# Two reorderings in the recurrent steps of a hybrid decoder: ScalarE's copy of the turned keys and VectorE's choice of levels

## The reference, cut to what matters

```python
def step(state, inp):                       # one chunk of one head
    qt, kt, vt, lf = inp
    b = jnp.cumsum(lf, axis=2)
    diff = b[:, :, :, None, :] - b[:, :, None, :, :]
    decay = jnp.where(tri, jnp.exp(jnp.where(tri, diff, 0.0)), 0.0)
    att = jnp.einsum('bhtc,bhsc,bhtsc->bhts', qt, kt, decay)
    o = jnp.einsum('bhts,bhsv->bhtv', att, vt) + jnp.einsum('bhtc,bhcv->bhtv', qt * jnp.exp(b), state)
    b_last = b[:, :, -1:, :]
    new_state = state * jnp.exp(b_last[:, :, 0, :, None]) + jnp.einsum('bhsc,bhsv->bhcv', kt * jnp.exp(b_last - b), vt)
    return new_state, o
```

## Time and profile before

| | us |
|---|---|
| median of 3 runs | 2272.9 (2272.58 to 2273.27) |
| the profiled execution | 2272.83 |
| its span in the profile | 2271.0 |
| TensorE busy | 2218.8 (98%) |
| TensorE weight loads busy | 1789.6 (79%) |
| VectorE busy | 1136.0 (50%) |
| ScalarE busy | 867.4 (38%) |
| GpSimd busy | 155.1 (7%) |
| mean granted TensorE clock | 0.996 |

### The profile page before, as it was taken

The page is one execution under the profiler, slowest core; times in us unless marked ns, Lnnn a source line. Parts: engine busy times, 40 slices in busy tenths (PEclk is TensorE's granted clock), DMA queues, the critical chain, the costliest instruction groups (busy, mean ns, idle before and its releaser), DMA issues.

```text
span 2271.0 us, 29054 instructions
## 1 busy us (share of the span) xinstructions
PE 2218.8 (98%) x11971; PEld 1789.6 (79%) x11971; DVE 1136.0 (50%) x1802; ACT 867.4 (38%) x1321; POOL 155.1 (7%) x136
## 2 busy tenths in 40 slices
PE   7999999999999999999999999999999999999998
PEld 6888887877667888888888888878776778888887
DVE  4333344888767333343643333458887563333444
ACT  3232223555655323222532322245565453222234
POOL 0000021211001000011000000212200010000210
PEclk9999999999999999999999999999999999999999
DMA  5333333322212333333333333323222233333322
GB/s 154 101 95 97 92 93 89 97 57 76 75 43 79 112 98 97 99 92 98 92 94 96 99 93 93 93 73 98 75 63 65 70 86 100 93 102 98 90 86 70
DMA packets 383443, 202.65 MB, mean 89 GB/s; under 512 B 17104, under 2 KB 380496, under 8 KB 383312
## 3 DMA queue, kind: packets, MB, share of 16 engines
q1 hardware_dynamic: 383312, 200.80, 30.8%
HBM read 198.68 MB, written 2.10 MB: 88 GB/s over the span
## 4 chain that ended last, share of the span: by engine, by line
PE 85%; DVE 7%; ACT 3%; issue 2%; DMA 1%; SPq 0%; DVEq 0%; ACTq 0%
PE banks L246 24%; PE banks L247 24%; PE banks L248 24%; PE banks L273 2%; PE banks L274 2%; PE banks L279 2%; DVE lev L1019 1%; DMA w_raw<-in_cmp_v_w_dram 1%; PE banks L1281 1%; DVE att L1055 1%; PE banks L1268 1%; DVE w_lo L238 1%; PE banks L1302 1%; PE banks L1232 1%; ACT lev L909 1%
## 5 line engine op out<-in xcount | busy, mean ns | idle before, releaser
L238 DVE TENSOR_TENSOR w_lo<-w_raw,w_hi 128x1024 fp32r<-128x1024 f32 (+2 forms) x378 | 457.3, 1214 | 867.5 <-ACT w_hi L232 867.1
L246 PE MATMUL banks<-xhi,w_hi 128*128 128x512 f32 x1888 | 743.4, 394 | 1.4 <-DVE proj L991 1.1
L248 PE MATMUL banks<-xhi,w_lo 128*128 128x512 f32 x1888 | 735.8, 390 | 0.0
L247 PE MATMUL banks<-xlo,w_hi 128*128 128x512 f32 x1888 | 735.4, 390 | 0.0
L232 ACT ACTIVATE w_hi<-w_raw 128x1024 fp32r<-128x1024 f32 (+2 forms) x378 | 377.1, 1000 | 854.0 <-PE banks L248 830.2
L246 PEld LDWEIGHTS banks<-xhi,w_hi 128*128 128x128 f32 x1888 | 356.4, 189 | 77.5 <-issue 2.5
L248 PEld LDWEIGHTS banks<-xhi,w_lo 128*128 128x128 f32 x1888 | 354.5, 188 | 74.7
L247 PEld LDWEIGHTS banks<-xlo,w_hi 128*128 128x128 f32 x1888 | 354.8, 188 | 72.8 <-issue 1.4
L246 PE MATMUL banks<-hhi,w_hi 128*128 128x512 f32 x704 | 277.4, 394 | 0.0
L248 PE MATMUL banks<-hhi,w_lo 128*128 128x512 f32 x704 | 274.1, 389 | 0.0
L247 PE MATMUL banks<-hlo,w_hi 128*128 128x512 f32 x704 | 274.0, 389 | 0.0
(11 more groups left out here) (247 smaller groups left out, 1953.6 us busy)
## 6 DMA issues: line engine op xcount, KB each, us to landing
w_raw<-in_ffn_w_gu_dram SPq DMA_DIRECT2D x176, 512.0 KB, 3.9
w_raw<-in_ffn_w_down_dram SPq DMA_DIRECT2D x64, 512.0 KB, 3.6
w_raw<-in_w_in_dram SPq DMA_DIRECT2D x48, 512.0 KB, 4.1
w_raw<-in_ffn_w_down_dram SPq DMA_DIRECT2D x32, 384.0 KB, 3.2
w_raw<-in_w_out_dram SPq DMA_DIRECT2D x32, 256.0 KB, 3.0
w_raw<-in_ple_gate_w_dram SPq DMA_DIRECT2D x16, 512.0 KB, 4.0
w_raw<-in_cmp_k_w_dram SPq DMA_DIRECT2D x8, 512.0 KB, 3.9
w_raw<-in_cmp_v_w_dram SPq DMA_DIRECT2D x8, 512.0 KB, 4.0
```

Source lines behind the costliest of these rows:

```text
L238: dve.tensor_tensor(part_view(wlo, n), raw_view(split_at[n]).rearrange("p k n -> p (k n)"), part_view(whi, n), ALU.subtract).then_inc(sems ...
L246: pe.matmul(bank, w_hi, x_hi, start=first, stop=False)
L247: pe.matmul(bank, w_hi, x_lo, start=False, stop=False)
L248: return pe.matmul(bank, w_lo, x_hi, start=False, stop=last)
```

## The change

Nothing is computed otherwise, and no instruction is added or taken away. Two pieces change places with their neighbours.

On ScalarE, in the third step of each of the first three heads (c = 2), the copy of the turned keys (line 954) now stands ahead of the next head's level exponentials (`part(h + 1, 2)`, lines 909 to 912) and no longer behind them.

On VectorE, in the first step of each of the first three heads (c = 0), `choose(n)` now stands ahead of the next head's first decay part (`part(h + 1, 0)`, lines 1000 to 1003) and no longer behind it.

```diff
@@ in_act @@
-                if -4 <= n < STEPS and c < 3 and h + 1 < H and n != -2:
+                of_next = -4 <= n < STEPS and c < 3 and h + 1 < H and n != -2
+                if of_next and c < 2:
                     part(h + 1, c)
...
                     act.activation(kd_t[:], ps[:, 4, 0:P], ACT.Copy).then_inc(sems["b4_out"], 1)
+                    if of_next and c == 2:
+                        part(h + 1, 2)
@@ in_dve @@
-                if -4 <= n < STEPS and h + 1 < H:
+                of_next = -4 <= n < STEPS and h + 1 < H
+                if of_next and (c or n < 0):
                     part(h + 1, c)
...
                 if 0 <= n < STEPS:
                     choose(n)
+                if of_next and c == 0 and n >= 0:
+                    part(h + 1, c)
```

## The result

The changed kernel takes 2278.8 us (median of 13 runs, 2276.6 to 2280.7) where the kernel before took 2272.9 us (13 runs, 2272.0 to 2275.8). The ratio is 1.0023, with a 95% interval of 1.0016 to 1.0031. It is slower, by 0.2%. The forecast was 2278.6 us.

What follows compares the result with a forecast made beforehand. Bound: one chain without play through VectorE and ScalarE, met by TensorE, 98% busy. Per layer 1.15 us delay plus 1.7 us half clock, 2 x 2.85 on 2272.83, gave 2278.5, stated as 2278.6 us; 8-in-10 range 2274.3 to 2283.0.

Steps and rivals of the forecast that it cites:

- TensorE's waits for `kd_t` go, and gain next to nothing: Line 832: waits of 0.77 us (step 3) and 2.02 us (step 11) vanish; chain shortens only 0.16 us in three heads.
- The wait for the scores: VectorE, step 0: the wait for `c_mm` now precedes the decay part, scores done at 439.12 where the part began at 438.67.
- The way to ScalarE and back: Line 1007 at least 4.90 us after line 1000; the 1.67 us choice leaves its room of 1.28, 1.30 and 0.69 us.
- Line 839: TensorE in steps 4, 8 and 12: starts at 468.42, 500.14 and 534.32, with new waits for `att` over 1 us.
- The clock: Falls to half once a layer, just before step 12, behind a wait of some 2.7 us, costing 1.7 us.
- The third rival: Clock also falls behind step 4's wait at line 839, doubling the scores' time: 1.2 us a layer, 2281.0 us; chance 20%.
- The sum: Both layers cost 2.85 us each, 5.7 us in all on 2272.83 us.
- The first rival: TensorE's waits and the half clock simply go: 4.5 us a layer faster, 2263.9 us; chance 6%.
- the second: No change: decay part's delay is taken up, only 0.5 us a layer gained; 2271.9 us, up to 2277; chance 19%.
- the three delays: Line 1007 later by 1.47, then 0.74, then 0.39 us in steps 0, 4 and 8, each less 0.16 at the next head.

Runs made afterwards that it cites:

- act_alone: Against the kernel before: only ScalarE's copy of the turned keys moved ahead of the exponentials, VectorE's order as before; 2273.2 us, ratio 0.9997.
- root_behind_split: Against act_alone: ScalarE's two root activations of the normalisation (steps 6 and 10) moved behind the next weight split; 2267.7 us, ratio 0.9972 to the kernel before.
- score_wait_first: Against act_alone: the decay part in steps 0, 4 and 8 also waits for the scores, choice still behind it; 2273.4 us, ratio 1.0004 to the kernel before.
- changed_again: The changed kernel measured and profiled once more, without any edit; 2278.1 us, ratio 1.0019 to the kernel before.
- changed_root_behind: Against the changed kernel: ScalarE's root activations moved behind the next weight split; 2273.7 us, ratio 0.9998 to the kernel before.
- dve_alone: Against the kernel before: only VectorE's choice moved ahead of the decay part in steps 0, 4 and 8, ScalarE's order as before; 2281.9 us, ratio 1.0038.
- choice_first_step0: Against the changed kernel: VectorE's choice goes first in step 0 only, steps 4 and 8 in the old order; 2275.2 us, ratio 1.0007 to the kernel before.

## Why the prediction was right, point by point

- **TensorE's waits for `kd_t` go, and gain next to nothing.** Right and shown: act_alone is 0.6 us a layer faster within the steps, and within its measurement the same. Of the rule of the Trainium skill ("Perfetto Trace Analysis", section Optimization Strategy) the runs show the limit: the dependency did start sooner, and the engine stood at the next one. Followed down to the chain behind that next one, the rule did give root_behind_split.
- **The wait for the scores.** Right, and score_wait_first shows it by itself: its decay part was expected 0.49 and 0.70 us later than before in steps 0 and 4 and came 0.48 and 0.76 later (438.45 and 468.09 against 438.67 and 468.03, less the 0.70 us by which that profile is early). Against act_alone this is 1.0 us at step 12. In the changed kernel line 1010 came 1.56 us later in step 0 (445.48 against 444.26, where this profile runs 0.34 us early, by line 832 of step 1) for 1.47 expected, and 2.23 in step 4 (476.12 against 474.23 less 0.34) for 2.05.
- **The way to ScalarE and back.** Right in mechanism and size: 4.90 us expected, 4.91 and 4.90 found, 0.37 us of delay in step 8 for 0.39.
- **Line 839.** Expected at 468.42, 500.14 and 534.32; found at 468.15, 499.95 and 534.12 in a profile that runs 0.34 early, so 0.1 us late each time. The chain's delay at step 12 was foreseen as 2.12 and is 2.27; with the clock 2.85 was foreseen, as 1.15 + 1.7, and 2.70 found, as 1.3 + 1.4. The waits came in another shape: the forecast had one of 2.7 us in step 12, and the trace has 1.14 us at line 837 for the state and 1.24 at line 839, since VectorE's update of the state stands on the same chain just before the choice.
- **The clock.** It fell behind step 12 in both layers, as foreseen. It also fell behind step 8 in the first layer and did no harm, as foreseen, but for another reason: TensorE didn't wait again in step 9 (line 839 at 508.53 without a wait); it was 0.2 us later there than in the second layer, which had no such fall, and its wait in step 12 took that up. The third rival (a fall behind step 4 makes the scores slower and the chain late with them) did not come true where it had the chance: changed_again had that fall in the second layer, and four steps on line 839 stood where the first profile had it (2.05 and 2.03 us later than before). The fall came only when the scores were nearly done, and so it was in the first layer of changed_root_behind. The mechanism itself is real: in the second layer of dve_alone the fall came one step earlier, the choice waited 2.44 us for the scores in place of 1.05, and the chain was 1.4 us later than in its first layer. What the prediction didn't have is the double stretch of the first profile, +1.3 us.
- **The sum.** 5.7 us were forecast as twice 2.85. The first profile has 2.7 + 4.0 in the two stretches, and 6.0 in the span. The remaining differences stand outside the steps: 0.3 us less before them, in the first layer 1.3 us more between 566 and 600 us, in the second 1.6 us less between 1685 and 1720, where the two profiles have their half clocks at other places (one more in the first layer, one fewer in the second). That part of the agreement is luck; the 2.7 is not. changed_again has 2.8 + 2.7 in the stretches.
- **The first rival (faster)** is excluded by act_alone, the second (nothing comes through) by choice_first_step0 and score_wait_first together with the changed kernel. The upper end that the prediction gave this second rival, 2277 us with one of the three delays, has no working: its largest single delay, 1.47 us less 0.16 three times, gives 2 x 1.0 us and 2274.9 us with the clock up, and choice_first_step0 measured 2275.2.

## What to carry to other kernels

Before a wait is taken from the busiest engine, look for the next meeting of that engine with the same partner, and how long ago its releaser ended there: 0.06 us of room at one line told here that 2.8 us of waits and a clock stretch were worth nothing. An instruction that hands work to another engine and gets it back needs its place kept by the length of the round trip (4.90 us here), whatever the work that could go ahead of it is urgent for. And a gap of an engine on such a chain isn't spare time: the gap's releaser, followed back two steps, pointed to 1.18 us of work on a third engine, in two places a layer. Moved behind the split, it gained 2.2 us a layer against act_alone, where the removal of TensorE's waits (5.6 us over the two layers) had gained nothing that the time could tell.

## What the runs showed of the hardware

The granted clock fell behind waits that were split in two, not only behind long ones: 1.14 and 1.24 us with a pair of small matmuls between them in step 12, where the kernel before had single waits of 1.04 us and 1.03 us (second layer) in step 9 and no fall behind them. The length of a wait alone doesn't tell. The wait of 1.24 us in step 4 of the changed kernel had no fall behind it in either layer of the first profile and one in the second layer of changed_again; waits of 0.88 and 1.24 us in step 12 had none in the first layer of choice_first_step0 and score_wait_first and one in the second; and of dve_alone's waits of 2.30 and 2.33 us in step 3 only the second had one. These windows belong to the two pairs of waits of choice_first_step0, in its first and its second layer:

```profile
533.00:537.00 4.00, 3.57 (x67) 2.95 (x68) 3.86 (x8) 1.85 (x4) 0.00 (x0) 1.00 0.00 0
...
1656.00:1658.00 2.00, 2.00 (x46) 1.72 (x39) 1.93 (x4) 0.92 (x3) 0.00 (x0) 0.50 0.03 8
```

So whether it falls at such a place differs from one layer and one execution to the next, and what decides it is open. The times of the changed kernel lie 4 us apart and most of those before, in the same series, within 1.3. This is not a mark of the changed order: in the later series the kernel before was itself spread over 5 us (2270.8 to 2275.9 in 27 runs). The longer runs mostly show the lower mean clock (2280.4 us at 0.992 and 2276.6 at 0.996 for the changed kernel, 2275.4 at 0.994 and 2270.8 at 0.997 for the one before), which fits falls that come and go; that they make the spread isn't shown.
